# Zero products, the bounds, a silu and the first experts: four edits to the prologue of a hybrid encoder step on Trainium2

## What is computed

```python
def reference(...):                      # for the prompt, then for the samples
    xn = rmsnorm(x, norm1)
    aq, af, ai, ag, bq, bk, bv, iq, ik, iw = split(xn @ w_in)
    f = lb + (1.0 - lb) * sigmoid(af)    # lb: softmax and cumsum of a_lb_raw
    # group A: gated recurrence S = diag(f) S + (1-f) i^T, o = S^T silu(aq)
    a_out = rmsnorm(a_o, a_gnorm) * silu(ag)
    # group B: indexer scores, top-k keys of each query, attention over them
    score = sum_h relu(iq_h . ik) * iw_h ; sel = top_k(score) ; b_o = softmax attention
    h = x + concat(a_out, b_o) @ w_o
    y = h + peer(rmsnorm(h, norm2))

def peer(xn):                            # per token and each of 8 heads
    q = xn @ wq                          # two halves of 64
    s = q . subkeys                      # (2, 128) scores
    sv, si = top_k(s, 16)                # the two lists
    cand = sv[0][:, None] + sv[1][None, :]        # 16 x 16 sums
    fv, fi = top_k(cand, 16)             # 16 of 16384 experts
    g = softmax(fv)
    return sum_k g_k * gelu(xn . u[e_k]) * v[e_k]
```

## Time and profile before

| | us |
|---|---|
| median of 3 executions | 1270.38 |
| lowest and highest | 1268.88, 1270.6 |
| the profiled execution | 1266.45 |
| its span, from the first instruction to the last | 1264.7 |

### The profile page before, as it was taken

The page is one execution under the profiler, slowest core; times in us unless marked ns, Lnnn a source line. Parts: engine busy times, 40 slices in busy tenths (PEclk is TensorE's granted clock), DMA queues, the critical chain, the costliest instruction groups (busy, mean ns, idle before and its releaser), DMA issues.

```text
span 1264.7 us, 11354 instructions
## 1 busy us (share of the span) xinstructions
PE 1060.4 (84%) x3313; PEld 518.5 (41%) x3313; DVE 794.4 (63%) x1941; ACT 356.7 (28%) x851; POOL 734.4 (58%) x774
## 2 busy tenths in 40 slices
PE   8999989997959988777989799878868777678885
PEld 4766555654326433333543354323223222223231
DVE  1649876989567588877627466666463556563334
ACT  2535215333133342232322333121221221222110
POOL 0005545666656666667656666666666666766654
PEclk9999989998989999989999999999998999999999
DMA  9958989999999999999999999999999999999997
GB/s 379 376 202 278 413 343 367 318 378 409 405 403 408 401 366 391 373 363 366 360 409 409 409 408 383 360 358 410 409 367 348 380 354 371 371 352 371 373 372 293
DMA packets 125629, 468.13 MB, mean 370 GB/s; under 512 B 14072, under 2 KB 17152, under 8 KB 123392
## 3 DMA queue, kind: packets, MB, share of 16 engines
q0 software_dynamic: 110592, 402.70, 83.2%
q1 hardware_dynamic: 14976, 64.70, 13.1%
HBM read 462.86 MB, written 4.42 MB: 369 GB/s over the span
## 4 chain that ended last, share of the span: by engine, by line
PE 43%; DMA 21%; POOL 13%; issue 9%; DVE 8%; another core or an unknown queue 4%; ACT 1%; POOLq 0%; DVEq 0%; SPq 0%; ACTq 0%
PE PSUM L1964 21%; DMA UV<-in_p_v,EIDX 15%; POOL UV L579 7%; PE PSUM L1544 6%; POOL UV L564 6%; DMA UV<-in_p_u,EIDX 5%; PE PSUM L1553 4%; PE PSUM L1743 3%; DVE UV L1461 3%; PE PSUM L1717 2%; PE PSUM L1558 1%; PE PSUM L1565 1%; PE PSUM L1760 1%; DVE SEL L213 1%
## 5 line engine op out<-in xcount | busy, mean ns | idle before, releaser
L1964 PE MATMUL PSUM<-UV,DIAG 128*128 128x512 f32 x1500 | 728.5, 618 | 152.8 <-DMA UV<-in_p_v,EIDX 119.6
L1461 DVE CUSTOM_DVE_ANT_0 UV<-UV,PSUM 128x1024 f32<-128x1024 f32 x384 | 463.6, 1218 | 313.6 <-DMA UV<-in_p_u,EIDX 259.6
L579 POOL DMA_INDIRECT UV<-in_p_v,EIDX x376 | 360.9, 960 | 278.3 <-PE PSUM L1964 140.8
L564 POOL DMA_INDIRECT UV<-in_p_u,EIDX x384 | 364.7, 950 | 237.1 <-issue 108.2
L1964 PEld LDWEIGHTS PSUM<-UV,DIAG 128*128 128x128 f32 x1500 | 267.3, 192 | 552.4 <-issue 274.1
L996 ACT ACTIVATE DIAG<-CST,WGT 128x128 f32<-128x128 f32 x375 | 143.5, 398 | 755.4 <-PE PSUM L1964 408.8
L1544 PE MATMUL PSUM<-WR,XW 128*128 128x512 f32 (+1 forms) x128 | 50.6, 555 | 0.1
L1553 PE MATMUL PSUM<-XW,WR 128*128 128x256 f32 x192 | 46.1, 398 | 3.7 <-issue 3.7
L1553 PEld LDWEIGHTS PSUM<-XW,WR 128*128 128x128 f32 x192 | 38.4, 201 | 12.4 <-issue 6.7
L1544 PEld LDWEIGHTS PSUM<-WR,XW 128*128 128x128 f32 x128 | 24.2, 190 | 25.3 <-issue 22.7
L1461 DVE DVE_READ_ACCUMULATOR2_ANT DOTS<- 128x1 f32 x384 | 31.6, 82 | 0.0
(11 more groups left out here) (286 smaller groups left out, 831.9 us busy)
## 6 DMA issues: line engine op xcount, KB each, us to landing
WR<-in_w_o SPq DMA_DIRECT2D x13, 512.0 KB
UV<-in_p_u,EIDX POOLq DMA_INDIRECT x384
UV<-in_p_v,EIDX POOLq DMA_INDIRECT x384
WR<-in_p_wq SPq DMA_DIRECT2D x10, 512.0 KB
UV<-in_w_o SPq DMA_DIRECT2D x2, 2048.0 KB, 12.1
UV<-in_p_wq SPq DMA_DIRECT2D x2, 2048.0 KB, 9.2
WR<-in_w_B SPq DMA_DIRECT2D x2, 2048.0 KB
UV<-in_w_B SPq DMA_DIRECT2D x4, 512.0 KB, 6.5
```

The lines of the kernel that those rows point to most:

```text
L564: nc.gpsimd.indirect_dma_start(UBUF[n % RU], None, a["p_u"], bass.IndirectOffsetOnAxis(EIDX[:, n:n + 1], 0)).then_inc(u_got[n % RU], 16)
L579: nc.gpsimd.indirect_dma_start(VBUF[m % RV], None, a["p_v"], bass.IndirectOffsetOnAxis(EIDX[:, n:n + 1], 0)).then_inc(v_got[m % RV], 16)
L1461: v.tensor_tensor_reduce(out=row, in0=row, in1=XNP, scale=1.0, scalar=0.0, op0=ALU.mult, op1=ALU.add, accum_out=DOTS[:, i % 2, s:s + 1]).t ...
L1964: ins = mm(bank[6 + k][:, :], DIAG[:, m % ND, :], VBUF[m % RV][:, k * 512:(k + 1) * 512], start=False, stop=m % SLOTS == SLOTS - 1 or m == ...
```

## The change

PE starts its eight products of zeros when their operand is zero, and waits for the identity behind them; the four products of zeros ahead of the first projection become two. The transpose of the bounds goes behind the second projection, and ACT takes the exponential behind the copies of `bp 0` and `bp 1`. ACT makes a one-element silu behind the numerators, copies `("gp", 0)` there, and makes a one-element sqrt behind `square_o(0)`. For tile 0 and head 0 the first eight experts come from the 8 x 8 sums of the two lists' first eight, before the lists' second eight are looked for.

```diff
 def product_order():
-    o = [...] + [("bp", 0, 0), ("lb",), ("bp", 0, 1), ("rb",), ("bp", 0, 2), ("fp", 0)]
+    o = [...] + [("bp", 0, 0), ("bp", 0, 1), ("lb",), ("rb",), ("bp", 0, 2), ("fp", 0)]
 
-def top16(own, v, rows, slot, pace):
-    for step in range(5):
+def top16(own, v, rows, slot, pace, steps=range(5)):
+    for step in steps:
 
 # scalar engine
             squares(0, X[0], JUNK)
+            out_bp0(0)
+            out_bp1(0)
             act.wait_ge(lb_shift, 1)
             own.done(nc.scalar.activation(SMALLC[:, 16:24], SMALLC[:, 16:24], ACT.Exp), lb_exp)
-            out_bp0(0)
-            out_bp1(0)
...
             numerators(0, 1, 0)
+            own.done(nc.scalar.activation(SMALLC[:, 73:74], STD1[:, 0:1], ACT.Silu))
+            copy_out(("gp", 0), SG[0], heads4, func=ACT.Silu)
             out_pt(0, 0, 0)
             out_pt(0, 1, 0)
             square_o(0)
-            copy_out(("gp", 0), SG[0], heads4, func=ACT.Silu)
+            own.done(nc.scalar.activation(SMALLC[:, 73:74], STD1[:, 0:1], ACT.Sqrt))
             copy_out(("pv", 0), MIXB, heads4)
 
 # vector engine, choose(t, h)
-                yield from top16(own, v, [... both lists ...], slot, 5)
+                lists = [... both lists ...]
+                if (t, h) == (0, 0):
+                    yield from top16(own, v, lists, slot, 5, range(2))
+                    own.caught_up()
+                    own.mark(v.tensor_copy(SIF[:, :, 0:8], SIU[:, :, 0:8].bitcast(U32)))
+                    few = SCORE[:, 0:64]
+                    own.done(v.tensor_tensor(few.rearrange("p (i j) -> p i j", i=8), wide(SV[:, 0, 0:8], 2, 8), wide(SV[:, 1, 0:8], 1, 8), ALU.add))
+                    own.done(v.max(FV[:, 0:8], few))
+                    own.done(v.max_index(FI[:, 0:8].bitcast(U32), FV[:, 0:8], few))
+                    yield from decode(t, h, 0, 8, slot + 1, 3)
+                    yield from top16(own, v, lists, slot, 5, range(2, 5))
+                else:
+                    yield from top16(own, v, lists, slot, 5)
...
                 if (t, h) == (0, 0):
-                    own.done(v.max(FV[:, 0:8], row))
-                    own.done(v.max_index(FI[:, 0:8].bitcast(U32), FV[:, 0:8], row))
-                    yield from decode(t, h, 0, 8, slot + 1)
                     own.done(v.match_replace(out=row, in_to_replace=FV[:, 0:8], in_values=row, imm_value=PICKED))
...
-            def decode(t, h, lo, hi, slot):
+            def decode(t, h, lo, hi, slot, bits=4):
# with bits=3 the place among 64 sums is split at 8, and the one-hot
# comparison, product and sum cover 2 x 8 x 8 elements instead of 2 x 8 x 16
 
 # tensor engine
-            pe.wait_ge(id_in, 16)
             pe.wait_ge(att_zero, 1)
             idle(8)
+            pe.wait_ge(id_in, 16)
             pe.wait_ge(x_in[0], 16)
...
-            idle(4)
+            idle(2)
             stored(pe, ("xt", 0, 0))
             rows_of(("bp", 0, 0), XNT2, weights("B0"))
+            rows_of(("bp", 0, 1), XNT2, weights("B1"))
             pe.wait_ge(lb_in, 16)
             pb = start(("lb",))
             end(nc.tensor.transpose(pb[:, 0:8], LBRAW, IDENT[0:8, 0:8]), ("lb",))
-            rows_of(("bp", 0, 1), XNT2, weights("B1"))
```

More of the change, by code:

```diff
@@ L81, in product_order @@
 def product_order():
-    o = [("xt", 0, g) for g in range(2)] + [("bp", 0, 0), ("lb",), ("bp", 0, 1), ("rb",), ("bp", 0, 2), ("fp", 0)]
+    o = [("xt", 0, g) for g in range(2)] + [("bp", 0, 0), ("bp", 0, 1), ("lb",), ("rb",), ("bp", 0, 2), ("fp", 0)]
     o += [("ti", 0), ("tk", 0), ("qp", 0)] + [("dt", 0, par, 0) for par in range(2)] + [("tq", 0), ("vp", 0)]
@@ L1239, in choose @@
                 stored(dve, ("se", t, h, 1))
-                yield from top16(own, v, [(SS[:, h, c, :], SV[:, c, :], SIU[:, c, :].bitcast(U32)) for c in range(2)], slot, 5)
+                lists = [(SS[:, h, c, :], SV[:, c, :], SIU[:, c, :].bitcast(U32)) for c in range(2)]
+                if (t, h) == (0, 0):
[10 more added lines that the diff above has]
+                    yield from top16(own, v, lists, slot, 5)
                 yield slot + 1
@@ L1258, in choose @@
                 yield from decode(t, h, 8 if (t, h) == (0, 0) else 0, PK, slot + 2)
-            def decode(t, h, lo, hi, slot):
-                k, n = slice(lo, hi), hi - lo
-                own.mark(v.tensor_scalar(FPART[:, 0, k].bitcast(U32), FI[:, k].bitcast(U32), 4, None, ALU.logical_shift_right))
-                own.mark(v.tensor_scalar(FPART[:, 1, k].bitcast(U32), FI[:, k].bitcast(U32), PK - 1, None, ALU.bitwise_and))
+            def decode(t, h, lo, hi, slot, bits=4):
+                k, n, j = slice(lo, hi), hi - lo, slice(0, 1 << bits)
+                own.mark(v.tensor_scalar(FPART[:, 0, k].bitcast(U32), FI[:, k].bitcast(U32), bits, None, ALU.logical_shift_right))
+                own.mark(v.tensor_scalar(FPART[:, 1, k].bitcast(U32), FI[:, k].bitcast(U32), (1 << bits) - 1, None, ALU.bitwise_and))
                 own.caught_up()
                 own.done(v.tensor_copy(FPF[:, :, k], FPART[:, :, k].bitcast(U32)), top_ready if hi == PK else None)
-                iota = wide(wide(IOTA, 1, n), 1, 2)
-                own.done(v.tensor_tensor(OH[:, :, k], wide(FPF[:, :, k], 3, PK), iota, ALU.is_equal))
+                iota = wide(wide(IOTA[:, j], 1, n), 1, 2)
+                own.done(v.tensor_tensor(OH[:, :, k, j], wide(FPF[:, :, k], 3, 1 << bits), iota, ALU.is_equal))
                 if n == PK:
                     yield slot + 1
-                own.done(v.tensor_tensor(OH[:, :, k], OH[:, :, k], wide(SIF, 2, n), ALU.mult))
-                own.done(v.tensor_reduce(EPART[:, :, k], OH[:, :, k], axis=AX, op=ALU.add))
+                own.done(v.tensor_tensor(OH[:, :, k, j], OH[:, :, k, j], wide(SIF[:, :, j], 2, n), ALU.mult))
+                own.done(v.tensor_reduce(EPART[:, :, k], OH[:, :, k, j], axis=AX, op=ALU.add))
                 at = slice((t * PH + h) * PK + lo, (t * PH + h) * PK + hi)
```

## The result

| | before | after |
|---|---|---|
| median of 20 executions each | 1268.83 | 1266.67 |
| lowest and highest | 1265.62, 1272.64 | 1262.34, 1270.66 |
| the profiled execution | 1266.45 | 1268.31 |
| its span | 1264.7 | 1266.5 |

The measured ratio is 0.9977 with an interval of 0.9966 to 0.9987: the change saves 0.23%, 2.9 us (1.6 to 4.3). The two medians themselves differ by 2.16 us, which lies inside that interval, so 2 to 3 us is as much as these runs say. The forecast was 3.3 us.

The account below looks back on a forecast made before the run. PE's chain in the prologue was taken to set the pace up to POOL's wait at 177.76. Zeros 2.9 plus silu 0.4 made 3.3 us, so 1270.4 - 3.3 = 1267.1 us, range 1264.6 to 1269.7.

Parts of the forecast that it names:

- What bounds the kernel: Prologue up to POOL's wait at 177.76: PE decides, only what moves PE counts, and its 3.3 us passes to the end.
- Zeros while the rows land: PE's start: zeros at 1.05, transposes at 4.64, first projection at 6.7; with AF's landing as limit, `fp` 2.9 us sooner.
- The rival of a later rise: PE's clock rises later, some 3 us more at the lower level: gain only 2.3 to 2.6 us; chance 0.12.
- The bounds behind the second projection: PE zero; on DVE `XNT0` ready at 25.7, 0.4 ahead of AF, so no cost; without AF's limit 0.1 to 0.2.
- a sign of being wrong: At `fp`: the forecast would be wrong if `fp` waited for line 1407 (DVE) instead of AF.
- Silu sooner: ACT before the output projection: silu load hidden in idle time, `MIXB` and output projection 0.4 us sooner, `MIXA` 1.7.
- The first eight experts: DVE's first choice: first numbers 2.4 us sooner, first dot product 0.5; for the end zero to 0.5.
- AQ: Rival: AQ's earlier request shares the DMA with AF, `fp` 2 us later than today, time 1272; chance 0.05.
- The stall in the trunk: Rival: PE's stall at 166.70 and slow products vanish, up to 4.7 us more, 1262 to 1265; chance 0.07.
- The zeros did start sooner: Answers the rival that something else holds PE until 4.5, leaving 0.4 + 0.4, time 1269.6; chance 0.04.
- Sum: Whole kernel: 2.9 + 0.4 = 3.3 us for PE at 116.14 and all behind it, giving 1267.1.
- The chance of "faster": Whole kernel: gain above 0.2%, about 2.5 us, given 0.68: forecast 0.60, half of one rival, another rival, less 0.03.

Follow-up runs that it names:

- late20: The changed kernel with 95 products of zeros instead of 2 ahead of the first projection; ratio to the kernel before 1.0142 (1.0111 to 1.0173).
- after_again: The changed kernel, unaltered, measured and profiled a second time on another comparison's chip; ratio to the kernel before 0.9995 (0.9975 to 1.0016).
- lb_early2: Second run of the changed kernel with the bounds' product back between the first two projections and LBRAW requested ahead of B1; ratio to before 0.9989 (0.9974 to 1.0005).
- cold: The changed kernel without any products of zeros ahead of the first projection; ratio to the kernel before 0.9995 (0.9979 to 1.0011).
- no_silu: The changed kernel with gp's silu copy back behind square_o and without the two one-element operations; ratio to the kernel before 0.9985 (0.9969 to 1.0001).
- no_first8: The changed kernel with the first eight experts taken from the 256 sums again; ratio to the kernel before 0.9980 (0.9967 to 0.9993).
- only_zeros: The kernel before with only the first edit, the earlier and fewer zeros; ratio to the kernel before 0.9989 (0.9967 to 1.0011).
- no_bounds: The changed kernel with the bounds' transpose back between the first two projections and the exponential ahead of the copies; ratio to before 0.9991 (0.9974 to 1.0008).
- lb_early: The changed kernel with the bounds' product back between the first two projections and LBRAW requested ahead of B1; ratio to the kernel before 0.9970 (0.9946 to 0.9993).

## Why the prediction was right, point by point

**What bounds the kernel.** Right as far as the runs resolve. The prologue's chain passes through: 2.56 us at `fp`, 2.85 at `wo`, 3.43 at the trunk, 3.24 at POOL's long wait, 2.9 (1.6 to 4.3) by the ratio, 2.2 and 2.5 by the medians of the two comparisons, and `late20` shows the slope for a long delay. Of the 3.43, some 0.5 is the single execution: from the first `qq` product to the trunk there are 26.77 us here (85.94 to 112.71), 26.35 and 26.77 in `after_again` and `lb_early2`, but 27.2 to 27.3 in the seven other profiles with the new choice, and 27.35 before.

**Zeros while the rows land.** Right in each step up to the first projection, to within 0.4: zeros at 1.00 (1.05), transposes at 4.84 (4.6), first projection at 7.07, waiting 0.63 for B0 (6.7). The projections run at the full clock. `cold` shows that this is what the edit is worth. The Trainium skill, TensorE: Matmul & The Clock Gate, "What's actually happening", says that the moment of the rise varies between executions, and the traces agree: the same eight zeros take 3.19 to 3.60 us in different profiles, and the eight transposes behind them 1.04 to 1.97. But in all the profiles with the earlier zeros the first projection had the full clock, 7.0 to 7.1 us for 16 products. The rival of a later rise did not come.

**The bounds behind the second projection.** The step that failed. "On PE it is the same product at another place: zero" was read from a trace in which PE came to it after its operand. The raw bounds' landing, some 16 us, stood in no row that I had read, and I had moved everything ahead of it by 3 us without asking whether this product would have to wait. In its old place it waits 1.5 to 1.9 us, and in one of two such executions the clock fell behind the wait, for another 1.7. What I priced at nothing saves 1.3 and 3.1 us at `fp` (27.60 and 29.96 against 26.32, the second less 0.5 for B0's later landing). It didn't spoil the sum, since the sum was made for all edits together, with the product where the change puts it; it would have spoiled a forecast for the first edit alone, for which my text gives 2.9 and the run 1.3.

On DVE I said that the move costs nothing while AF is the limit, 0.1 to 0.2 without it. In the profile of the changed kernel it costs 0.45. The row of 3.8 us was right but started 0.5 later than reckoned: the copies of the second projection end at 22.40, not at 21.9, as the projections themselves ran 0.5 later. `XNT0` came at 26.27 instead of 25.7, and AF at 6.24 + 19.6 = 25.84 instead of 26.1. So `fp` waited for line 1419 (line 1407 of before), which I had named as a sign of being wrong. That sign comes and goes: in `no_silu` and `no_first8`, which have the same order here, `fp` waited for AF, as forecast, and there the move cost nothing. The two limits lie within 0.5 us, hence the start of `fp` at 26.32 was only 0.17 off the 26.15; that it came so close with the other limit deciding is luck.

The Trainium skill, ScalarE: Activation LUTs, "What ACT_TABLE_LOAD costs", gives every switch a drain of 1.38 us beside the load. Here the load starts 0.03 behind the copy ahead of it (21.93 + 0.47 to 22.43), the exponential 0.01 behind the load's end, and the next load 0.02 behind the exponential. No drain is to be seen; by the page `XNT0` would have been ready at 27.65.

**Silu sooner.** Right: 0.3 to 0.4 at `wo`, wait 0.93 to 0.43. `MIXA` is ready at 74.76 + 0.69 = 75.45, and isn't waited for.

The same profile, ACT's row behind the copy of `gp`:

```profile
65.14 0.60 ACT L602 ACTIVATE SG<-PSUM 128x512 f32<-128x512 f32 x1 [3.83 <-PE PSUM L1570]
...
67.73 1.28 ACT L955 ACT_TABLE_LOAD   x1
69.03 0.20 ACT L955 ACTIVATE SMALL<-SMALL 128x1 f32<-128x1 f32 x1
69.26 0.60 ACT L602 ACTIVATE MIXB<-PSUM 128x512 f32<-128x512 f32 x1
```

The silu copy has left the row behind `square_o`, and in its place stands the 0.20 of the one-element sqrt: 0.60 - 0.20 is the saving.

**The first eight experts.** Right on DVE: 3.61 us instead of 6.03, 2.42 sooner for 2.4 forecast; first gather 5.28 sooner (5.7); from the start of the choice to the first dot product 19.21 us instead of 20.02, 0.8 less for 0.5 forecast. The fifth gather came 4.5 sooner, not 3.3: before, it was held for 1.13 us by something that the profile marks as remote, not by PE, as I had put it; after, it waits 1.95 for PE. For the end both are worth the same, nothing that the runs resolve.

**Rivals.** AQ, asked for at 14.20 instead of 17.22, took nothing from AF, which landed at 25.84 (before 6.12 + 20.0 = 26.12), and AQ itself landed at 30.8 (14.20 + 16.6; before 17.22 + 13.8 = 31.0): the order of the requests decided, as the text argued. The stall in the trunk stayed. The zeros did start sooner.

**Sum.** 2.9 + 0.4 = 3.3 was forecast; 2.56 + 0.3 = 2.85 is in the rows up to `wo`, 2.9 in the ratio, 2.2 in the medians. Of the 0.45 between 3.3 and 2.85, 0.17 is the later `fp` (26.32, not 26.15), 0.18 the base that I took for it (29.06, the modelled end of the products before it, where it starts at 28.88), and 0.1 the silu. The absolute time, 1266.67 for 1267.1 forecast, is nearer than the sum deserves, and that is luck: the start from 1270.38, a median of three executions, was 1.55 above the 1268.83 of twenty, and the 3.3 is 1.1 more than the two medians differ by. The chance of "faster" has a slip: by its own terms it is 0.60 + 0.06 + 0.07 - 0.03 = 0.70, not 0.68.

**What stays open.** Why the clock falls in one execution and not in another with the same work, and why the rate of the transfers between 500 and 800 us differs by 2% between two profiles. Whether the bounds' move gains or loses anything against the earlier request can't be told by these runs, nor whether all of the prologue's gain arrives at the end.

## What to carry to other kernels

When an edit starts an engine sooner, list every operand that it meets on the new way with its landing time, the small ones above all: 4 KB asked for behind 2 MB of weights land behind them, and a row without a wait shows only that the engine came later than its operand. An edit that looks idle alone may be what makes another one pay, so undo edits singly and add them singly before one is dropped. And where single executions spread by 8 us, read a gain of 3 from the marks at which its chain passes, in more than one profile, and take one large delay as a check of the slope, which is only as sharp as its interval.

## What the runs showed of the hardware

- **The granted clock in the record doesn't show the start.** In `cold` the window from 8 to 10 us says 1.00 with 4 products in 2 us, and that from 14 to 16 says 1.00 with 6. The pace of the products tells the level, the record only later drops: at 18 to 20 us in `no_bounds` it says 0.50, with the same 4 products. In both windows a product takes 1.06 us (median), against 0.59 at the full clock.
- **One drop of the clock is as large as the whole change.** In two of 14 profiles (`after_again`, `lb_early2`) it fell to 0.50 between 54 and 60 us, behind a stretch with PE partly idle, and cost 1.5 and 3.2 us at the output projection; in the other twelve it stayed up in that stretch, or at least the 44 us from `fp` to `wo` show nothing of it (43.7 to 44.2).
- **A small transfer landed behind the large ones asked for ahead of it**: 4 KB asked for behind B1 at 4.82 us (`only_zeros`) landed at 15.84, asked for at 5.55 (`no_bounds`) at 16.50, and ahead of B1 at 3.55 (`lb_early`) in time for PE at 14.23. The request in `lb_early`:

```profile
3.55 0.38 SPq L471 DMA_DIRECT2D WR<-in_lbraw  x1
```
- **A table load is followed by the next operation at once**, 0.01 and 0.02 us behind its end in the rows above (22.43 + 1.28 to 23.72, 67.73 + 1.28 to 69.03).
